# A two-part network on one core: the last product of a layer in two passes, four weight buffers and six smaller moves

## The reference, cut to what matters

```python
# first block: two layers over 256 latent rows h and 256 context rows hc, D = 2048
for l in range(2):
    shift, scale, gate = jnp.split(silu_c @ w_mod[l] + b_mod[l], 3, axis=-1)   # the same for the context
    n  = rms_norm(h,  pre_norm_g[l]) * (1.0 + scale)  + shift
    nc = rms_norm(hc, pre_norm_g[l]) * (1.0 + scale_c) + shift_c
    p  = jnp.split(n @ w_in[l], split_points, axis=-1)                           # 13 parts; pc from nc
    oa, oa_c = diff_attention(...)        # p = softmax(...); a = p[0] - lam * p[1]; rms_norm(a @ v) * (1 - lambda_init)
    ob, ob_c = window_attention(...); on, on_c = neighborhood_attention(...)
    od, od_c = qknorm_attention(...)      # q and k rms-normed by head, then rotated
    y  = (jnp.concatenate([oa, ob, on, od], -1) * jax.nn.silu(p[12])) @ w_out[l]
    h  = h  + gate   * rms_norm(y,  post_norm_g[l])
    hc = hc + gate_c * rms_norm(yc, post_norm_g[l])                              # layer 0 only
# second block: h = 16 meta rows and the 256 rows
z = rmsnorm(h, mix_norm) @ w_in; u, q_a, kv_a, k_pe = ...
ya = s5_mixer(u, ...)        # associative_scan; g = gelu(y); out = g * sigmoid(g @ w_glu + b_glu)
yb = mla_mixer(q_a, kv_a, k_pe, ...)   # 8 heads, chunk-causal softmax(q_nope k_nope + q_pe k_pe) v
h = h + jnp.concatenate([rmsnorm(ya, out_norm_ssm), rmsnorm(yb, out_norm_attn)], -1) @ w_out
h = h + conv_ffn(rmsnorm(h, ffn_norm), w_up, conv_w, conv_b, w_down)             # 5504 wide
return rmsnorm(h, final_norm)[:, 16:]
```

## Time and profile before

| what | value |
|---|---|
| median of 3 runs | 3235.52 us (3230.89 to 3237.34) |
| the profiled execution: its own time, its span | 3228.44 us, 3226.4 us |
| mean granted PE clock | 0.949 of full speed |
| PE busy | 2951.7 us, 91% |
| DVE busy | 1938.9 us, 60% |
| ACT busy | 1135.1 us, 35% |
| HBM traffic | 148 GB/s over the span |

### The profile page before, as it was taken

The page is one execution under the profiler, slowest core; times in us unless marked ns, Lnnn a source line. Parts: engine busy times, 40 slices in busy tenths (PEclk is TensorE's granted clock), DMA queues, the critical chain, the costliest instruction groups (busy, mean ns, idle before and its releaser), DMA issues. The chain is left out here.

```text
span 3226.4 us, 40361 instructions
## 1 busy us (share of the span) xinstructions
PE 2951.7 (91%) x15557; PEld 2383.0 (74%) x15557; DVE 1938.9 (60%) x3393; ACT 1135.1 (35%) x1800; POOL 401.7 (12%) x397
## 2 busy tenths in 40 slices
PE   7979998999889987989998899979979999999998
PEld 2447677877667876768776778755778999999887
DVE  3228778676767665362443557876845666666444
ACT  3222332323223324232342443333334444444443
POOL 5760000000100000000001004543400000000000
PEclk9989999999889998999999989975989999999999
DMA  8846245252434653232322454420334555545555
GB/s 324 275 139 220 79 138 199 104 175 95 135 131 156 211 204 131 92 105 95 118 101 92 139 171 135 132 70 22 125 105 145 172 174 183 175 165 173 191 193 167
DMA packets 151393, 480.60 MB, mean 149 GB/s; under 512 B 17040, under 2 KB 18064, under 8 KB 150032
## 3 DMA queue, kind: packets, MB, share of 16 engines
q1 hardware_dynamic: 138816, 435.22, 39.7%
q10 hardware_dynamic: 9824, 33.88, 2.8%
q0 software_dynamic: 2560, 8.91, 0.9%
HBM read 464.84 MB, written 13.11 MB: 148 GB/s over the span
## 5 line engine op out<-in xcount | busy, mean ns | idle before, releaser
L1428 DVE TENSOR_TENSOR split_weights<-common,split_weights 128x1024 fp32r<-128x1024 f32 x636 | 789.6, 1251 | 707.7 <-ACT split_weights L2136 655.1
L2136 ACT ACTIVATE split_weights<-common 128x1024 fp32r<-128x1024 f32 x636 | 663.0, 1052 | 904.6 <-PE bank L1104 788.9
L1102 PE MATMUL bank<-split_weights,features 128*128 128x512 f32 x1920 | 807.8, 421 | 49.6 <-DVE first_block_work L1635 16.5
L1104 PE MATMUL bank<-split_weights,features 128*128 128x512 f32 x1920 | 761.1, 396 | 0.0
L1103 PE MATMUL bank<-split_weights,features 128*128 128x512 f32 x1920 | 760.8, 396 | 0.0
L1102 PEld LDWEIGHTS bank<-split_weights,features 128*128 128x128 f32 x1920 | 368.1, 192 | 166.7 <-issue 55.8
L1103 PEld LDWEIGHTS bank<-split_weights,features 128*128 128x128 f32 x1920 | 369.2, 192 | 78.7 <-issue 11.3
L1104 PEld LDWEIGHTS bank<-split_weights,features 128*128 128x128 f32 x1920 | 367.4, 191 | 80.4
L1102 PE MATMUL bank<-ffn_input_split,split_weights 128*128 128x256 f32 (+1 forms) x1376 | 395.7, 288 | 14.2 <-DVE split_weights L1428 13.0
L1104 PE MATMUL bank<-ffn_input_split,split_weights 128*128 128x256 f32 (+1 forms) x1376 | 390.6, 284 | 0.0
L1103 PE MATMUL bank<-ffn_input_split,split_weights 128*128 128x256 f32 (+1 forms) x1376 | 389.8, 283 | 0.0
(11 more groups left out here) (296 smaller groups left out, 3447.1 us busy)
## 6 DMA issues: line engine op xcount, KB each, us to landing
common<-w_in SPq DMA_DIRECT2D x260, 512.0 KB, 3.3
common<-w_up SPq DMA_DIRECT2D x172, 512.0 KB, 4.4
first_block_work<-w_mod_cols SPq DMA_DIRECT2D x256, 256.0 KB, 3.6
common<-w_out SPq DMA_DIRECT2D x96, 512.0 KB, 3.3
common<-w_down SPq DMA_DIRECT2D x84, 512.0 KB, 3.6
old_stream<-w_mod SPq DMA_DIRECT2D x64, 512.0 KB, 5.0
trig<-common ACTq DMA_DIRECT2D x32, 272.0 KB, 4.8
second_block_work<-trig POOLq DMA_DIRECT2D x32, 272.0 KB, 3.5
```

Of the source, the lines that this page charges most:

```text
L1102: e.matmul(out_ap, xs[0], ws[0], start=first, stop=False)
L1104: return e.matmul(out_ap, xs[0], ws[1], start=False, stop=last)
L1428: e.tensor_tensor(lo, raw, hi.bitcast(F32), ALU.subtract).then_inc(*low_done.tick(("lo", m)))
L2136: e.activation(split_slots[:, 0, i, 0:words], raw_slots[:, m % RAW, 0:words], ACT.Copy).then_inc(*high_done.tick(("high", m)))
```

## The change

- **Layer boundary.** In layer 0 the last `w_out` chunk is made twice over, first for the two latent tiles, then for the two context tiles, so its 8 weight pieces are loaded and split twice (104 loads of `w_out` for 96; `high` and `low` 640 for 632). The latent tiles' end (`stream_end`) is side work under the context pass. The context tiles' end and their features (`context_end`) are side work in layer 1's first q projection, and `normed` makes feature tiles of 128x256 by stream (32 splits on DVE and on ACT for 16 of 128x512).
- **Squares.** In the glu loop `sum_squares` of tile ct - 2 stands ahead of `glu` and `gained` of tile ct; in `add_projected` likewise for the ffn squares.
- **Turns.** `mla_turn` runs at x - 3 and `mla_values` at x - 4; `turn_pe` one product later, with two buffers `pe_tmps`.
- **Buffers.** RAW and HALVES are 4.
- **Softmax combination.** `combine` leaves the first map unnormalised and folds both factors into one pass; L1691 goes (16 of 128x512, 8 of 128x256), and `heads_out` scales EPS by the squared sum (12 small instructions of 128x4).
- **qk heads.** In `norm_heads` ACT copies the bank to `stage` and squares from there, and DVE multiplies out of `stage`, so the copy frees the bank. `keep_v` moves from DVE to ACT.
- **Second block's start.** `new_h` of layer 1 goes in halves (4 of 128x1024 for 2 of 128x2048), `h_turn` waits for its own half, and `second_loads` stands behind the `h_turn` loop. `scan_load` is issued from ACT's queue.

PE has 14658 instructions in both; DVE 3371 for 3395, ACT 1786 for 1684, POOL 369 for 401, SP 974 for 966. The core of the diff:

```diff
-RAW = 3
-HALVES = 3
+RAW = 4
+HALVES = 4
...
-        for c in range(4):
+        for c in (*range(4), 3)[:4 if l else 5]:
...
+            if c == 3 and l < DEPTH - 1:
+                self.project(tiles[:LT], self.y_rows(l, c, at))
+                self.feature_end[(l, 0)] = self.taken - 1
+                self.side_work.append(self.stream_end(l, 0))
+                self.pace = 1.0
+                self.project(tiles[LT:], self.y_rows(l, c, at))
+                self.feature_end[(l, 1)] = self.taken - 1
+                self.side_all()
+            else:
+                self.project(qtiles, self.y_rows(l, c, at))
+        if l == DEPTH - 1:
+            for t in qtiles:
+                self.do("row_scale", l, t)
+            for half in range(2):
+                for t in qtiles:
+                    self.do("new_h", l, t, half)
...
+    def stream_end(self, l, stream):
+        tiles = range(stream * LT, stream * LT + LT)
+        for step, at in (("row_scale", l), ("new_h", l), ("scale_rows", l + 1), ("rows_scaled", l + 1)):
+            for t in tiles:
+                self.do(step, at, t)
+                yield
+        if stream == 0:
+            self.do("keep_stream", l)
+
+    def context_end(self, l):
+        yield from self.stream_end(l - 1, 1)
+        for _ in range(CONTEXT_AFTER):
+            yield
+        yield from self.normed(l, 1)
...
-        self.do("second_loads")
         for f in range(KT):
             self.do("h_turn", f, 3 + f % 5, self.copies())
             self.gained("mix", f)
         self.gained_end()
+        self.do("second_loads")
...
+        def turn(wait):
+            if turns and turns[0][0] + wait < taken_by:
+                self.do("turn_pe", turns.pop(0)[1], self.next_acc())
         for grp in range(6):
             m = self.take()
             for s in range(2):
                 n = 2 * grp + s
                 bank = self.next_acc()
                 self.do("columns", ("q", n), bank, m, s * CH, 4, 0, 3, "qa", 0, Q0, T2, s == 1)
-                if turns:
-                    self.do("turn_pe", turns.pop(0), self.next_acc())
+                taken_by += 1
+                turn(0 if n < MH else 1)
...
-            if 0 <= x - 2 < units:
-                self.do("mla_turn", x - 2)
+            if 0 <= x - 3 < units:
+                self.do("mla_turn", x - 3)
             self.side(2.0)
-            if 0 <= x - 3 < units:
-                self.do("mla_values", x - 3)
-                if (x - 3) % 3 == 2:
-                    self.gained("attn", (x - 3) // 3)
+            if 0 <= x - 4 < units:
+                self.do("mla_values", x - 4)
...
             self.columns(("glu", ct), bank, 1, "g", 0, 0, TQ)
+            if ct > 1:
+                self.sum_squares("ssm", ct - 2, ST, 7)
             self.do("glu", ct, bank)
             self.gained("ssm", ct)
-            if ct > 1:
-                self.sum_squares("ssm", ct - 2, ST, 7)
...
+            if name == "ssm" and ct > 3:
+                self.sum_squares("ffn", ct - 4, KT, 7)
...
+            tb, part = banks[4 + f % 4], slice(stream * LAT, (stream + 1) * LAT)
+            for s, n in seen.new(at("normed_turned", l, f, stream), at("scales_ready", l),
+                                 at("feature", "normed", l, f - 2, stream) if f > 1 else START):
+                e.wait_ge(s, n)
+            e.tensor_scalar(probs_a[0][:, part], tb[:, part], scaled_g[l][:, f, stream:stream + 1],
+                            mod_all[l][:, f, stream:stream + 1], ALU.mult, ALU.add).then_inc(
+                *features_made.tick(("modulated", l, f, stream), ("free", "normed", l, f, stream)))
...
-            e.reciprocal(dd[:, 2:4], dd[:, 0:2]).then_inc(*probs_combined.tick())
+            sm = sums[t % 2][:, u % HEADS:u % HEADS + 1]
+            e.reciprocal(dd[:, 2:3], dd[:, 1:2]).then_inc(*probs_combined.tick())
             e.wait_ge(*probs_combined.last())
             for s, n in seen.new(at("lambda", l)):
                 e.wait_ge(s, n)
-            e.tensor_scalar(dd[:, 3:4], dd[:, 3:4], lam_col, None, ALU.mult).then_inc(*probs_combined.tick())
+            e.scalar_tensor_tensor(out=dd[:, 3:4], in0=dd[:, 2:3], scalar=lam_col, in1=sm, op0=ALU.mult, op1=ALU.mult).then_inc(
+                *probs_combined.tick())
             e.wait_ge(*probs_combined.last())
-            e.tensor_scalar(pb_, pb_, dd[:, 3:4], None, ALU.mult).then_inc(*probs_combined.tick())
-            e.wait_ge(*probs_combined.last())
-            e.scalar_tensor_tensor(out=pa, in0=pa, scalar=dd[:, 2:3], in1=pb_, op0=ALU.mult, op1=ALU.subtract).then_inc(
+            e.scalar_tensor_tensor(out=pa, in0=pb_, scalar=dd[:, 3:4], in1=pa, op0=ALU.mult, op1=ALU.subtract).then_inc(
                 *probs_combined.tick(("probs", u), ("probs_b", pb)))
...
+            e.activation(stage[t][:, 0:w], banks[bank][:, 0:w], ACT.Copy).then_inc(*heads_kept.tick(("free", "acc", p, t)))
+            e.wait_ge(*heads_kept.last())
+            for s, n in seen.new(at("turn", x - 2)):
+                e.wait_ge(s, n)
+            e.activation((turn_a, turn_b)[x % 2][:, 0:w], stage[t][:, 0:w], ACT.Square).then_inc(
...
+        def keep_v(l, g, width, p, t, bank):
+            for s, n in seen.new(at("acc", p, t), *part_free(l, g, "v")):
+                e.wait_ge(s, n)
+            names = [("free", "acc", p, t)] * (width == CH)
+            e.activation(v_rows1[:, t, 0:width], banks[bank][:, CH - width:CH], ACT.Copy).then_inc(
+                *heads_kept.tick(("head", l, g, "v", t), *names))
...
+        def scan_load(j):
+            for s, n in seen.new(at("table_stored", SJ - 2), at("table_stored", SJ - 1),
+                                 at("scan_out", j - TRIGS) if j >= TRIGS else START):
+                e.wait_ge(s, n)
+            e.dma_start(trig_bufs[j % TRIGS], A["trig"][j]).then_inc(*trig_loaded[j % TRIGS].tick(("trig", j)))
...
-            for s, n in seen.new(at("columns", "q", MH + i), at("pe_ready", i - 1 if i else "k")):
-                e.wait_ge(s, n)
-            e.activation(pe_tmp[:, 0:TQ], banks[bank][:, 0:TQ], ACT.Copy).then_inc(
+            for s, n in seen.new(at("columns", "q", MH + i), at("pe_ready", i - 2 if i > 1 else "k")):
+                e.wait_ge(s, n)
+            e.activation(pe_tmps[(i + 1) % 2][:, 0:TQ], banks[bank][:, 0:TQ], ACT.Copy).then_inc(
```

204 lines of the change are left out of this document (94 added, 110 removed).

## The result

The changed kernel takes 3153.05 us (median of 4 runs, 3149.87 to 3156.41) beside 3235.93 us for the kernel before on the same chip: a ratio of 0.9747, 95% interval 0.973 to 0.9764. The forecast was 3152, and the direction and the size came true. The stages did not: one term of the sum has the wrong sign, two (the turns and the qk heads) give next to nothing in place of -24, and the squares, the buffers and two smaller terms are larger by nearly as much. The profiled execution took 3150.2 us, its span is 3148.0, against 3228.44 and 3226.4.

A forecast was written before the change was run, and what follows sets the result against it. PE was taken to set the time, through 274.7 us idle and stretches at its lower clock. Nine terms summed to -83 from 3228.4, giving 3145.4, plus 7.1 for the median: 3152 us, range 3115 to 3205.

The forecast's parts named there:

- Layer boundary, -6: Last w_out chunk to first q projection: two passes turn 101.5 us into 94.7; -6 us taken (+4 to -14).
- the hole is filled: Layer boundary: the middle 25 us, where PE is busy 5.05 and waits 15.6 for row scaling, get filled.
- DVE bounds both: Layer boundary: DVE, not PE, sets the context pass (26.5 us) and the q projection (46.4 us).
- Turns, -10: Later turns remove the 7.2 us wait before turn_pe (-6) and the MLA units' 4.4 us start wait (-4); -5 to -15.
- table loads, +3: Scan steps: 32 load issues move from POOL to ACT, a tenth of a microsecond allowed each; +3 us (0 to +15).
- Squares, -22: Glu loop and ffn squares: earlier squares save 17 of 41 us in glu and 5 in ffn squares (-12 to -27).
- Buffers, -21: Weight low parts: a fourth buffer saves 12 us of ffn idle, 4 for the clock, 5 elsewhere (-8 to -28).
- 12 of the 15.7: Ffn: the fourth buffer removes 12 us of PE's 15.7 us idle time in 516.
- Softmax pass, -5: Attention units: dropping L1691's 0.49 us pass saves 4.9 us over the 10 waits behind it (-2 to -12).
- qk heads, -14: qk heads: ACT's copy frees the bank, saving 14 of 16.5 us in 5 PE waits (-8 to -18).
- The clock did not rise under the MLA units: Rival, chance 0.14: the clock rises under the MLA units, 55 us for 80, -25, giving 3127 us.
- The second rival: Rival, chance 0.22: gains are given back to DVE's backlog or the turn of the heads; only -30, giving 3205 us.

The follow-up runs named there:

- experiment 1: Changed kernel with the layer boundary as before (one pass of the last w_out chunk, no doubled loads, features of 128x512): 3143.67 us, ratio to before 0.9723.
- Experiment 2: Changed kernel with modulation's background pieces at every second instead of every third side step through layer 0's w_out chunks: 3188.04 us, ratio to before 0.9857.
- experiment 9: Changed kernel with turn_pe as early as before (after the next product), still with two buffers: 3149.89 us, ratio to before 0.9739.
- experiment 11: Changed kernel with mla_turn at x - 2 and mla_values at x - 3 as before: 3152.81 us, ratio to before 0.975.
- experiment 10: Changed kernel with each scan table's load, still on ACT's queue, two side steps later in the order: 3156.2 us, ratio to before 0.9755.
- experiment 4: Changed kernel with three raw and three split weight buffers again instead of four: 3190.22 us, ratio to before 0.987.

## Why the prediction was right, and where it was not

By the whole it was right through terms that missed on both sides. The sum was -83 from the profile; 78.2 came.

**Layer boundary, -6, measured +10.8 (9.4 by the medians of experiment 1).** The failed step is "the hole is filled". The sum had 21.8 + 26.5 + 46.4 = 94.7; the windows are 22.0 + 30.5 + 9.3 + 50.3 = 112.1. The 9.3 us are a hole between the context pass and the q projection, with PE busy 2.08 us, for which the sum had no term: four modulation pieces run in a row on DVE there, ahead of the first feature, and one waits 1.9 us for its weights. The count of pieces was nearly right for the rest, six and five against six and four, but not what a piece costs: none of their waits for DMA was in the sum, and in the whole stretch they are 9.1 us. The other two misses, 4.0 and 3.9 us, are in the context pass, where 3.4 us of these waits lie, and in the q projection. I took DVE's work from a list of instructions and their durations; the 18 pieces in the chunk before were in the trace too, but there DVE was busy 26.17 of 44 us and PE 43.83, so they cost nothing. Experiment 2 has the same passes and the doubled loads with no modulation: counted as the 101.5 us of the sum, from the first product to the end of the last, 93.9 us, where the step said 94.7 with eleven pieces. "DVE bounds both" was wrong as well for the q projection: it is busy 39.25 of 50.3 us, 78% and not the 95% I named as a sign, and takes turns with ACT at each feature pair (in the whole stretch 9.2 us in 12 waits for ACT's high part). I had kept this for the upper end (+4), and it is not enough.

**Turns, -10, and table loads, +3: measured +2 together.** "With two buffers and a product more it goes" failed: the product more undoes the second buffer (experiment 9). The units' waits of 7.7 us went as told and came back as a wait for POOL's scan step and as time at the lower clock (experiment 11). The sum had named the clock as open there; it moved the other way. For the table loads, "the slot should be free" with a lead of three steps was a misreading: load j waits for scan_out of j - 3, which in the list stands directly ahead of it. ACT waited 19 us, and it cost nothing that a later place would save (experiment 10). Their price alone was not run. The kernel before with four buffers and ACT's loads takes 5.2 us longer from the units to the glu products than the one before, with 9.8 us more at the lower clock and PE's gaps as they were. Three or four buffers make no difference there (0.0 between experiment 4 and the changed kernel), so the loads are what is left, above the forecast's 3 and not by holding ACT.

**Squares, -22, measured -28 to -30.** Right mechanism. The glu loop gave 21 us for the 17 forecast, since the clock came back fully, and the ffn squares 7.5 for 5 (their waits fell from 10.0 to 3.2 us). The upper end was 27.

**Buffers, -21, measured -37** (27 in the ffn, 10 elsewhere). The term mis-sized is "12 of the 15.7": idle time as the profile shows it was 57% of what was lost there (15.9 of 27.6), all of it went, and 8.5 us of hidden waits with it. The 4 for the clock were about right (3), the 5 elsewhere were too few.

**Softmax pass, -5, measured -8.6.** More than the ten waits that the profile gave to it, inside the ends of 2 and 12.

**qk heads, -14, measured -3 or less.** "The wait could return there" was written as a doubt, and it did, in full in layer 1. The end of 8 was too high. **v copies, -5,** about -12 by subtraction, not measured. **New rows, -3,** measured -2.0 at this wait (5.0 us for 7.0); the third microsecond of the stage comes in the products behind it.

**Rivals.** The clock did not rise under the MLA units: it was at its lower level for longer. The second rival was right that gains would be given back at the boundary and at the turn of the heads; but of the 35 us forecast for the first block 21.0 came, more than the third that it would leave, and buffers and squares gave more than planned. Table loads did hold ACT, 19.0 us in all, which was named as a sign of being wrong, but PE lost nothing by it that a later load would save. The signs: glu tile 3.4 us (4 or less), clock 1.00 there, ffn idle 2.4 of 487 (below 5 of 500), turns of the heads 42.9 + 12.6 and more, above the 50 named; waits for low parts 16.8, below 25; idle PE time 219.4, below 230. The whole came out one microsecond from the forecast, and that part is luck: the boundary, the turns with the table loads and the qk heads missed by some 37 us together, and the other terms made up for 32 of them.

## What to carry to other kernels

Before work is moved under a pass, count what already stands on that engine in the same stretch, background work above all, in the trace and not in the list of what moves: here the modulation pieces cost nothing under a full pass with DVE busy 60% of it, and PE's time wherever the edits put them (packed into the w_out chunks: 48 us for 24 more; spread over the attention stages: 16 us for 34 more). A second buffer and a later consumer of it cancelled each other here; make one of the two edits and look before the other. And for a PE-bound stretch measure start to start: the idle time that a profile shows misses waits shorter than the drawn length of a matmul. Last, price the clock stage by stage: behind the gaps of the glu loop it cost 9 us beside 12 of idle time, behind the gaps of the ffn 3 beside 24.

## What the runs showed of the hardware

- Matmuls of 256 to 258 columns start 0.12 us apart at the higher clock and are drawn 0.28 us long, so that waits up to 0.16 us can't be seen as idle: about 8.5 us in the ffn before.
- In the glu stretch gaps of 1.88 us at each of the tiles (one of 2.90) went with a granted clock of 0.79; without them it was 1.00, and 155 matmuls in 41 us became 157 in 20. In the ffn before, behind gaps of the same size (1.84 and 1.86) between unbroken rows of products, the clock fell twice, for 3.4 us each time; behind three gaps of 1.67 to 1.70 it did not.
- Under the MLA units PE is busy 105.96 of 109 us at 0.50. With 8.5 us fewer gaps from there to the glu products the time at 0.50 was 120.0 us instead of 109.8.
- Outside the edited stages two kernels' matmuls keep their distance to 0.1 us over hundreds of microseconds in the later part of the program; of the distance between runs up to 4.6 us arise in the first 350, and up to 3 more until the end of the layer boundary.
